# Dilated attention in steps of two units, with the first output products inside the last group

## What is computed

```python
# q, k, v: 3 groups (dilations 1, 4, 16) x 8 heads x 64, each normalised and rotated
for g, (window, dilation) in enumerate(((128, 1), (512, 4), (2048, 16))):
    s = einsum(q_block, [previous k_block, k_block]) / 8   # blocks of 128 queries
    s = where(0 <= dist <= 128, s, -1e30)
    e = exp(s - max(s)); o[g] = (e / sum(e)) @ [previous v_block, v_block]
    lse[g] = max(s) + log(sum(e))
w = softmax(lse over groups)
y = sum(w[g] * o[g]) * silu(gate)
x = x + y @ w_out                                  # 512 -> 1024
```

## Time and profile before

| | |
|---|---|
| median of 3 runs | 2580.75 us (2577.23 to 2582.17) |
| the profiled execution's own time | 2577.0 us |
| its span in the profile | 2575.2 us |
| TensorE (PE) busy | 2436.3 us, 95% of the span |
| VectorE (DVE) busy | 1580.5 us, 61% |
| ScalarE (ACT) busy | 1052.3 us, 41% |
| GpSimd (POOL) busy | 931.6 us, 36% |
| dilated attention, first scores to last output product of the fourth slice | about 613 to 1261 us of the span |

### The profile page before, as it was taken

How to read it: one execution, slowest core, us unless ns; L and a number is a source line. 1 busy time by engine, 2 the same in 40 slices (tenths; PEclk the granted TensorE clock), 3 DMA queues, 4 the chain that set the end, 5 groups by cost and what they waited for, 6 DMA issues and landing times. The chain is left out here.

```text
span 2575.2 us, 31714 instructions
## 1 busy us (share of the span) xinstructions
PE 2436.3 (95%) x11542; PEld 1879.3 (73%) x11542; DVE 1580.5 (61%) x2033; ACT 1052.3 (41%) x1655; POOL 931.6 (36%) x525
## 2 busy tenths in 40 slices
PE   7999999999999999999799999999989999799996
PEld 5877648886776676766678777787768888688785
DVE  6999963466545454464665655444577777536774
ACT  5555671334443444354343223222344344333343
POOL 2888902332222122212132121222235455454443
PEclk9999999999999999999999999999999999899998
DMA  3111152221111111111022111221125665776763
GB/s 128 42 49 44 69 189 98 90 85 40 40 38 30 38 38 41 36 33 46 17 82 80 49 37 42 76 66 41 49 99 142 152 163 135 222 284 217 254 233 110
DMA packets 112516, 239.81 MB, mean 93 GB/s; under 512 B 42504, under 2 KB 45448, under 8 KB 112392
## 3 DMA queue, kind: packets, MB, share of 16 engines
q1 hardware_dynamic: 73440, 217.33, 26.2%
q10 hardware_dynamic: 38952, 20.76, 3.6%
HBM read 185.49 MB, written 46.27 MB: 90 GB/s over the span
## 5 line engine op out<-in xcount | busy, mean ns | idle before, releaser
L743 POOL CAST w_hi<-w_raw 128x1024 fp32r<-128x1024 f32 x98 | 107.4, 1096 | 1187.8 <-PE ps_A L835 526.0
L736 POOL TENSOR_TENSOR w_lo<-w_raw,w_hi 128x1024 fp32r<-128x1024 f32 x124 | 312.4, 2519 | 55.5 <-ACT w_hi L1417 47.6
L835 PE MATMUL ps_A<-HA_hi,w_hi 128*128 128x512 f32 x640 | 209.0, 408 | 23.5 <-POOL w_lo L736 15.6
L800 POOL TENSOR_TENSOR down_w_lo<-d_raw,down_w_hi 128x512 fp32r<-128x512 f32 x112 | 164.3, 1492 | 179.8 <-ACT down_w_hi L2063 179.8
L835 PE MATMUL ps_B<-HA_hi,w_hi 128*128 128x512 f32 x640 | 206.2, 403 | 3.6 <-DVE G L2188 3.3
L835 PE MATMUL ps_A<-HA_lo,w_hi 128*128 128x512 f32 x640 | 198.9, 392 | 0.0
L835 PE MATMUL ps_A<-HA_hi,w_lo 128*128 128x512 f32 x640 | 198.3, 391 | 0.0
L835 PE MATMUL ps_B<-HA_lo,w_hi 128*128 128x512 f32 x640 | 197.9, 391 | 0.0
L835 PE MATMUL ps_B<-HA_hi,w_lo 128*128 128x512 f32 x640 | 197.6, 390 | 0.0
L2960 DVE TENSOR_TENSOR ht_lo<-t_raw,ht_hi 128x1024 fp32r<-128x1024 f32 x56 | 84.5, 1547 | 113.4 <-ACT ht_hi L2047 113.4
L835 PEld LDWEIGHTS ps_A<-HA_hi,w_hi 128*128 128x128 f32 x640 | 115.3, 189 | 52.6 <-issue 28.5
(11 more groups left out here) (450 smaller groups left out, 5972.8 us busy)
## 6 DMA issues: line engine op xcount, KB each, us to landing
w_raw<-w_dram SPq DMA_DIRECT2D x124, 512.0 KB, 3.3
d_raw<-w_dram SPq DMA_DIRECT2D x64, 512.0 KB, 5.0
t_raw<-u_dram SPq DMA_DIRECT2D x56, 512.0 KB, 6.8
a_raw<-w_dram SPq DMA_DIRECT2D x32, 512.0 KB, 7.6
u_dram<-b SPq DMA_DIRECT2D x56, 256.0 KB, 4.6
u_dram<-t SPq DMA_DIRECT2D x48, 256.0 KB, 6.8
X<-x_dram SPq DMA_DIRECT2D x16, 512.0 KB, 6.8
d_raw<-w_dram SPq DMA_DIRECT2D x32, 256.0 KB, 3.0
```

What stands on the lines that cost most here:

```text
L736: pool.tensor_tensor(w_lo[q][:, :, :], w_raw[q][:, :, :], w_hi[q][:, :, :].bitcast(F32), ALU.subtract).then_inc(S[f"w_ready{q}"], 1)
L743: pool.tensor_copy(w_hi[q][:, :, :], w_raw[q][:, :, :]).then_inc(S["w_rounded"], 1)
L800: pool.tensor_tensor(lo[:, :, :], d_raw[i % 3][:, down_parts(x), :], hi[:, :, :].bitcast(F32), ALU.subtract).then_inc(S["down_split"], 1)
L835: op = pe.matmul(AB[b][:, cols], wt[:, w0 + k, :], act[:, k, cols], start=(first and k == ks[0] and step == 0), stop=(last and k == ks[-1] ...
```

## The change

Units are taken two at a time; a **step** s is units 2s and 2s + 1, and a group has 4 steps.

- TensorE: the scores of both units go into one PSUM tile (unit i at column 256 i of each half), with one `scores_done`. Both units are turned into one tile C or D (up to 8 transposes, one `turned`), and both units' values go into its first 256 columns (one `unit_done`). Two slices of the next weight tile stand between steps.
- ScalarE: one copy per step of up to 1024 columns into one buffer `pt` that is no longer doubled; for s >= 1 it waits for the `unit_done` of the step before. The copy of step s - 1 now stands ahead of the exponentials of step s.
- VectorE: both units' `softmax_input` follow one `scores_done`; `scores_out` is still given per unit. One `take_out` of 256 columns per step.
- The last group of the last pair gets a `carry` of its own, `first_out`: slices 0 and 1 of the first output tile stand where slices 5 and 7 would, slice 2 between the last turn and the last values. The group now waits for that tile's weights and for its PSUM tile at its start. The third turn of the shares follows the second directly.
- `YS_lo` now lies over `y_at` itself, `YS_hi` over q_in, k_in and the two rotary tables; so `split_ys` moves into the group, after the second, third and fourth step's `softmax_input`.

Cut to its core:

```diff
-        pt = [at_k.take(f"pt{i}", [P, 4 * P]) for i in range(2)]
-        YS = split_pair("YS", HB0 + 32 * KB, PAIRS)
+        pt = Region(nc, (ra.at, ra.at + 4 * KB)).take("pt", [P, 8 * P])
+        YS = (Region(nc, (HB0 + 32 * KB, HB0 + 48 * KB)).take("YS_hi", [P, PAIRS, T], F32R),
+              Region(nc, (HB0, HB0 + 16 * KB)).take("YS_lo", [P, PAIRS, T], F32R))
...
 # tensor
-                for u in range(BLOCKS):
-                    if q is not None:
-                        op = products(tile, q, HA, [u], first=(u == 0), last=(u == KT - 1))
...
-                    if u >= 2:
-                        values(u - 2)
-                    if u >= 1:
-                        turn_probs(u - 1)
...
+                carry(tile, [0])
+                pe.wait_ge(S["qk_ready"], n.next("qk_ready"))
+                pe.wait_ge(S[f"ab_free{other}"], n.now(f"ab_free{other}"))
+                scores(0)
+                turn(lambda c: vT[:, c * P:(c + 1) * P], BLOCKS)[1].then_inc(S["v_turned"], 1)
+                carry(tile, [1, 2])
+                turn_probs(0)
+                for s in range(1, STEPS):
+                    if s > 1:
+                        if s < STEPS - 1:
+                            values(s - 2)
+                        turn_probs(s - 1)
+                    pe.wait_ge(S["scores_out"], n.next("scores_out", 2))
+                    scores(s)
+                    if s < STEPS - 1:
+                        carry(tile, [2 * s + 1, 2 * s + 2])
+                values(STEPS - 3)
+                carry(tile, [KT - 1])
+                pe.wait_ge(S["scores_out"], n.next("scores_out", 2))
+                def rest(k):
+                    if k == 2:
+                        values(STEPS - 2)
+                        turn_probs(STEPS - 1)
+                    if k == 4:
+                        values(STEPS - 1)
...
+            def first_out(tile, ks):
+                for k in ks:
+                    if k in (5, KT - 1):
+                        out_part(tile, 0, 0, [(k - 5) // 2])
...
                 if last:
-                    rest = dilated(ORDER[2], None)
-                    rest(3)
-                    rest(5)
+                    rest = dilated(ORDER[2], 0, first_out)
+                    rest(2)
+                    out_part(n.ab ^ 1, 0, 0, [2])
+                    rest(4)
...
             turn_share(0)
             turn_share(1)
-            out_part(b0, 0, 0, range(PAIRS - 1))
             turn_share(2)
 # scalar
+                for s in range(1, STEPS):
+                    if queries and s == 2:
+                        after_ab()
+                        square("q", q_in, q_sq)
+                    if queries and s == 3:
+                        gain("q", q_in)
+                    between(s)
+                    copy_turned(s - 1)
+                    probabilities(s)
 # vector
+                softmax_input(0)
+                softmax_input(1)
+                between(0)
+                take_out(0)
+                softmax_input(2)
+                between(1)
+                softmax_input(3)
+                take_out(1)
+                between(2)
...
             shares()
-            for k in range(PAIRS - 1):
-                split_ys(k)
```

More of the change, by code:

```diff
@@ L1005, in neighbourhood, with dilated, turn_probs @@
                 return rest
-            def dilated(g, q):
+            def dilated(g, q, carry):
                 slots = {}
[L1013 to L1016, removed]
+                def turn_probs(s):
+                    slots[s] = b = take_cd()
+                    at = 0
+                    for u in step_units(s):
+                        pe.wait_ge(S["probs_ready"], n.next("probs_ready"))
+                        nk, rows = attn_keys(g, u)[1], sc[u % 2]
+                        for c in range(2 * nk):
+                            op = pe.transpose(CD[b][:, at:at + P], rows[:, c // nk, c % nk * P:(c % nk + 1) * P], ident[:, :])
+                            at += P
@@ L1058, in dilated @@
[L1058 to L1067, removed]
+                    at = 0
+                    for i, u in enumerate(step_units(s)):
+                        k0, nk, _ = attn_keys(g, u)
+                        for c in range(nk):
+                            for h in range(2):
+                                d = slice(HD * h, HD * h + HD)
+                                op = pe.matmul(CD[slots[s]][d, i * P:(i + 1) * P], V[:, k0 + c, d],
+                                               pt[:, at + (h * nk + c) * P:at + (h * nk + c + 1) * P],
+                                               start=(c == 0), stop=(c == nk - 1))
+                        at += 2 * nk * P
@@ new lines, in values, with scores @@
+                    op.then_inc(S["unit_done"], 1)
+                pe.wait_ge(S[f"w_ready{q}"], n.next(f"w_ready{q}"))
+                tile = take_ab()
+                other = tile ^ 1
+                def scores(s):
+                    for i, u in enumerate(step_units(s)):
+                        k0, nk, _ = attn_keys(g, u)
+                        for h in range(2):
+                            rows, at = slice(HD * h, HD * h + HD), h * HALF + 2 * i * P
+                            op = pe.matmul(AB[other][:, at:at + nk * P], qT[rows, u * P:(u + 1) * P],
+                                           kT[rows, k0 * P:(k0 + nk) * P], start=True, stop=True)
+                    op.then_inc(S["scores_done"], 1)
@@ new lines, in dilated, with next_tile, carry @@
+                values(STEPS - 3)
[7 more added lines that the diff above has]
+                        values(STEPS - 1)
+                return rest
+            def next_tile(q):
+                def carry(tile, ks):
+                    for k in ks:
+                        op = products(tile, q, HA, [k], first=(k == 0), last=(k == KT - 1))
+                        if k == KT - 1:
+                            op.then_inc(S[f"lin_done{q}"], 1)
+                return carry
@@ L1123, in _ @@
             pair(last=True)
-            def out_part(b, t, half, ks):
-                for k in ks:
-                    pe.wait_ge(S["ys_ready"], k + 1)
-                    op = products(b, t, YS, [k], w0=half * PAIRS, first=(k == 0), last=(k == PAIRS - 1))
-                return op
             def out_half(t, half):
@@ L2450, in pair @@
                     evacuate(k_in[:, :], g)
[L2451 removed]
+                    take_out(2)
                     rope("q", q_in, qT)
[L2453 removed]
+                    take_out(3)
                     rest()
```

174 lines of the change are left out of this document (70 added, 104 removed).

## The result

The changed kernel takes 2536.22 us (median of 4 runs, 2534.09 to 2538.34) against 2578.99 for the kernel before on the same chip (4 runs, 2575.41 to 2582.17): a ratio of 0.9833, 95% interval 0.9821 to 0.9846. The profiled execution took 2534.09 us, its span is 2532.3.

The account below looks back on a forecast made before the run. TensorE, busy 95% of the span, bounds the kernel, so only idle time and seams can be won. Groups 14 + 2.5 + 12 - 1.5 + 1 = 28 us, last group 1.5, rounded to 29: 2580.75 - 29 = 2551.7 us, range 2544 to 2569.

Parts of the forecast that it names:

- rival A: The forecast itself, gains in the carrying groups and the last group as summed: 2545 to 2558 us, chance 0.52.
- Scores show no such part (0.42 narrow, 0.63 wide by the same rows): Eleven carrying groups: score calls on TensorE have no fixed cost of their own, so joining them gains nothing.
- Seams and values: Carrying groups: four fewer departures from the product stream, 0.8 us a group; four fewer value calls, 0.6 us a group.
- Turns: Carrying groups: transposes of probabilities, 0.19 us for two, at most 0.85 for eight in a row; returns 0.1 us a group.
- the pause: Carrying groups' end: TensorE's wait for the last softmax_input before the next linear goes, gaining 2.5 us in all.
- The waits for the copy: Carrying groups: TensorE's 23 waits for copied probabilities, 11.5 us, vanish; 12 us gained, cover just even at wide groups' step 2.
- the tight places: Carrying groups: single pt buffer, last copy behind DMA issues, and step 2 of wide groups; 1.5 us charged.
- rival B: Waits come back at step 2's turn and the last values: eleven groups lose 14 us, 2566 us; chance 0.24.
- rival D: Softmax chain longer than the slices covering it, stopping in-order TensorE: 41 us lost against 28 gained, 2592; chance 0.05.
- The start of a pair: First turn after gated (3.25 us on VectorE): TensorE waits 0.95 us against 1.3 lost before; +1 us for three pairs.
- The last group: Dependent chain: steps of 5 to 5.5 us, last take_out 1.5 us later, tail behind it 15.1 instead of 18.2; gain 1.5 us.
- Rival C: Tail: nearly 3 us idle before y's fourth slice drops TensorE to half clock, losing 1 to 2 us: 2555; chance 0.14.

Follow-up runs that it names:

- split_scores: Changed kernel with both units' scores issued in two calls, at steps 2 and 3 with the turn between them: 2541.33 us, 0.9853 of the kernel before.
- less_cover: Changed kernel with one slice instead of two between step 2's scores and turn, slice 6 moved beside slice 7: 2545.72 us, 0.9868 of the kernel before.

## Why the prediction was wrong, point by point

**The sign, the mechanism and rival A** were right; the size was off by 14 us, half as much again.

**The step that failed is the sentence "Scores show no such part (0.42 narrow, 0.63 wide by the same rows)".** I had split the values into a part by size and a part by call from two shapes, 0.37 and 0.59. By the same split the scores give 0.63 - 0.42 = 0.21 for twice the columns, hence 0.42 - 0.21 = 0.21 by call: the rows held the term, and I read past it. It was worth 9 us (44 calls at 0.20 in `split_scores`, at 0.19 to 0.21 in the account), and without it the time would have been about 2545, inside the range. The row of the scores in the account has 1.8 us more, which the waits behind them had cost; of this I had 0.5, in the 12 us of the waits.

**Seams and values** came nearly as forecast: 9.8 for 8.8, 6.7 for 6.6. In `slices` there are 44 visits fewer, so a seam is 0.22 us.

**Turns** were mis-sized the other way. The 0.19 us of the earlier trace rows was the distance to a slice, and ahead of a slice the forecast was right: eight take 0.85. But the change puts 33 of the 44 turns ahead of scores, where each takes 0.12 to 0.18 us more. The forecast had the turns 1.4 us cheaper with the pause taken in, they became 3.8 dearer: 5.2 us against me, half of what the scores' row brought. The five misses (10.8, 1.0 and 0.1 for me, 5.2 against, 1.9 for me in the waits) make the 8.6 us by which the groups beat the forecast.

**The waits for the copy** went, 13.4 us with the pairs' starts for 11.5. The turn of step 2 waits for nothing in the carrying groups, and "just even" in a wide group was right to 0.2 us, as `less_cover` and the row of 721.95 show; the 1.5 us charged for the tight places were not needed. So rival B (0.24) and rival D (0.05) did not come, by a narrow margin in the wide groups: the same mechanism starts as soon as one slice is moved.

**The start of a pair** was right. `gated` takes 3.25 us again, and the first turn waits in two parts, 0.41 + 0.55 = 0.96 us, for the 0.95 of the walk; in the other two pairs it waits 0.80 and 0.48. Timelines of DVE and PE, against the earlier trace rows:

```profile
770.29 3.25 DVE L2477 TENSOR_TENSOR y_at<-O,y_at 128x1024 f32 x1
```

```profile
775.71 0.44 PE L1025 MATMUL ps_C<-ident,sc 128*128 128x128 f32 x2 [0.41 <-ACT sc L1654]
776.69 0.66 PE L1025 MATMUL ps_C<-ident,sc 128*128 128x128 f32 x4 [0.55 <-ACT sc L1654]
```

The Trainium skill (SBUF — State Buffer, on the shared port pair) has the two operations exclude each other, so the overlap with GpSimd was to stay. The trace agrees: GpSimd's split of weights runs from 770.10 for 2.36 us, and `gated`, begun beside it at 770.29, ends 1.08 us after it; the 3.25 us is unchanged.

**The last group** was walked too slowly. I had steps of 5 to 5.5 us and the last `take_out` 1.5 us later; the steps are 4.7, and it came 1.9 us sooner than in the first profile of before, 3.4 better than the walk. The evacuation of the gate was right (1.48 for 1.4), so was the way behind it: 15.5, 14.4 and 15.8 us for 15.1.

**Rival C** came in part. Behind the last slice of y the clock was at the 1.2 GHz level in all three profiles of the changed kernel, and 1.3 to 2.1 us went there. The idle stretch I named (nearly 3 us) was 2.75 to 3.56. It did not decide the time, since the groups brought so much. The Trainium skill (TensorE: Matmul & The Clock Gate, Part 1) says that sustained activity releases the throttled level; that the carried slices so keep the clock up within the group agrees with the ten profiles that carry them, from the first of them on. Ahead of it the clock fell in the third profile of the changed kernel (0.54 from 1186 to 1188), where no slice stands yet.

**The signs named.** From one group's turn of v to the next one's, a narrow group became 2.8 us shorter (2 to 2.5 were named), a wide one 3.3 to 3.9 (2.5 to 3.5), a mixed one 3.6 to 4.3. The last slice of y came 4.7 us sooner instead of 1 to 2.

**Together**, first profile against first profile, the span is 42.9 us shorter: 36.1 up to the end of the last linear, 4.7 from there to the last slice of y, 2.1 lost to the clock, 4.2 behind the attention. The last is code that the change doesn't touch, and I had nothing for it. That part takes 1262.7 and 1263.9 us in the two profiles of before, and 1258.2 to 1262.8 in the twelve of the changed kernel and its variants, 1260.4 in the mean. So some 1 to 2 of the 4.2 us are scatter, and 2 to 3 may belong to the change. About 1.2 us of it is a shorter wait in the neighbourhood attention: 4.0 and 4.2 us in two waits in the profiles of before, 2.8 or 2.9 in all three of the changed kernel:

```profile
PE ps_A L991 <- DVE nvT L2568: 2.9, 2, 1.8
```

Why it is shorter, and where the rest comes from, is not shown.

## What to carry to other kernels

When small operations are joined, split every kind's time into a part by size and a part by call from two shapes before calling one of them free: here each joined call of fp32 scores or values saved 0.15 to 0.2 us, while a turn cost 0.12 to 0.18 us more ahead of scores than ahead of a slice. Read seams as the distance over the pair of neighbours as it will stand after the change, not as it stands now. Count the cover of an in-order engine's wait in the slices that stand before it: with two of them the softmax chain was hidden, in the wide groups by 0.2 us or less, and with one it cost 11 us. And read such a margin from the length of the whole group: the brackets held only half of the cost.

## What was not expected of the hardware

A call of two or four small fp32 products costs 0.2 us beyond its columns though no wait is recorded and TensorE counts as busy; of the 36 us that left the groups, 21 left busy time. A wait costs more than its bracket: the scores ahead of one take 0.07 us longer. Ahead of the slices of y the granted clock fell behind 2.38 to 3.56 us of idle in eight profiles of eight and behind 2.2 us in one of four; yet ahead of the first share turn, behind 3.34 us and more, it stayed up in two of fourteen, and behind 1.33 and 0.48 us in the last group it fell in one execution and not in another of the same kernel. And stretches of 566.3 us repeat to 0.1 us between chips, while those with idle TensorE scatter by 2 us and more.
